# Two up projections of a decoder trunk, from plain 512-token products to 2x2 blocks with seven half-size products

## The chip, the cores and the metric

The kernel runs as one program on one core of a Trainium2 chip. The metric is the device time of that core in microseconds. TensorE (PE) multiplies, ScalarE (ACT) and VectorE (DVE) read PSUM and work elementwise, GpSimd (POOL) works elementwise on SBUF alone, SyncE (SP) issues nearly all transfers.

## The reference

A two-layer decoder trunk on 512 tokens with a model width of 1024, all in float32. Layer 0 mixes with block-sparse and dilated attention, layer 1 with stick-breaking attention; after each mixer comes a gated MLP, and after both x becomes LayerNorm(alpha * x + f(x)). What is changed is the first matrix product of the MLP in both layers (F = 2816):

```
def conv_ffn(h, w_up, conv_w, conv_b, w_down):
    u = h @ w_up                          # 512 x 1024 times 1024 x 5632
    up = pad(u, two rows of zeros in front)
    c = conv_b + sum over j of conv_w[j] * up[:, j:j + S]      # causal, width 3, per column
    g, val = c[..., :F], c[..., F:]
    return (silu(g) * val) @ w_down
```

## The kernel before

Every float32 product is three fp32r matmuls: each operand is split into a head (`w_hi`, `xt_hi`: the value rounded to fp32r) and a rest (`w_lo`, `xt_lo`: what the rounding left), and a product is hi*hi + lo*hi + hi*lo. The weights come as one stream of 1024 KB steps (two units of 128x1024), each into one of two buffers `w_raw`. For each step SP issues the load once POOL has made the rests of the step two before (`load`, L197), ACT copies the whole step into `w_hi` (`heads`, L301, one instruction at L305), and POOL subtracts twice 128x1024 into `w_lo` (`rest`, L242, L248). PE waits for each unit's rest.

The up projection keeps the activations transposed: `xt_hi` and `xt_lo` hold 8 chunks of 128 input columns by 512 tokens. There are 22 pairs f of a gate tile and a value tile, each 128 output columns by 512 tokens, one weight step for each pair. `col_unit` (L885, matmuls at L897) makes one tile with 8 chunks x 3 matmuls of 512 tokens, 48 for a pair. The first two pairs are cut into token halves of 256 (`first_columns` at L903, `up_half` at L1159), woven into the transposes of the norm before; `up_body` (L1149) does the other 20. Gates go to PSUM banks 0 and 2, values to 1 and 3. For each tile ACT makes the last tap and the bias from PSUM (L499, L505), DVE adds two more taps from PSUM (L795, L799), ACT takes a sigmoid (L503), and DVE multiplies twice (L805, L809) into `h_all`. ACT has in its order also the heads of the pair two ahead. The down projection then reads `h_all` in 11 chunks of two tiles (heads L490, rests L817) with matmuls at L866 into all eight banks; `row_tiles` (L845) takes the four token tiles of a chunk one after the other, 12 matmuls each.

Ahead of the up projection stands `norm` (L623): per token tile a sum (L576), statistics (L604 to L610), the scaled result (L596, L619), then PE transposes it (`turn_x`, L841) into PSUM, ACT copies heads (`xt_heads`, L314) and DVE makes rests (`xt_rests`, L564). Each engine's order is written out by hand; all waits are semaphores. ACT's queue issues the gains and shifts of the norm (`load_gain`, L309). No transfer is issued by POOL.

Of the kernel before, what the change touches and what calls it, by code (L numbers as in the profile page):

```python
# [22 lines left out]
F32 = mybir.dt.float32  # L23
# [38 lines left out]

WARM = (20, 5)


def build(nc, x_in, w_stream, ident_in, rope_in, mask_in, tri_in, conv_in, ln_in, out):
    ctx = ExitStack()
    with ctx:
# [13 lines left out]
        xt_lo = sb("xt_lo", [P, KD, S], F32R)  # L82
        a_hi = sb("a_hi", [P, KD, S], F32R)
        a_lo = sb("a_lo", [P, KD, S], F32R)
        x = sb("x", [P, NT, D])
        gain = sb("gain", [P, D])
# [25 lines left out]
        with ExitStack() as st:  # L112
            h_all = sb("h_all", [P, KF, S], stack=st)
            cg, cv, sig = ([sb(f"{n}0", [P, S], stack=st)] for n in ("cg", "cv", "sig"))
            sb("below_second", [P, S], stack=st)
            for n, tiles in (("cg", cg), ("cv", cv), ("sig", sig)):
                tiles.append(sb(f"{n}1", [P, S], stack=st))
        with ExitStack() as st:
# [43 lines left out]

        V = [Phase(f"v{l}", "rows act dve") for l in range(DEPTH)]
# [3 lines left out]
        N = [Phase(f"n{i}", "rows sum mean sq lv y0 va nt mulg xn scaled shifted") for i in range(2 * DEPTH)]  # L167
        T = [Phase(f"t{i}", "mm hi lo") for i in range(2 * DEPTH)]
        U = [Phase(f"u{l}", "g_mm cg cv g1 gc sg m1 v1 vc h") for l in range(DEPTH)]
# [10 lines left out]
        def filled(c, it):  # L180
            return 16 * (c // 2 + it + 1)


        @block.sync
        def _(sp):
# [11 lines left out]
            def load(c, it=0):  # L197

                sp.wait_ge(lo_ready, 2 * (c + 2 * it) - 2)
                sp.dma_start(w_raw[c % 2][:, :], w_stream[c + 2 * it]).then_inc(raw_full[c % 2], 16)  # L200

# [22 lines left out]
            with sp.Fori(0, (STEPS - ahead - 7) // 2) as it:  # L224
                for j in range(2):
                    load(ahead + 7 + j, it)
            for t in range(NT - 1):
                if t < 2:
                    sp.wait_ge(N[-1]["shifted"], t + 1)
# [11 lines left out]
        def _(pool):  # L241
            def rest(c, it=0):  # L242
                s = c % 2
                for u in range(2):

                    pool.wait_ge(hi_ready, 2 * (c + 2 * it) + u + 1)
# [14 lines left out]
            for l in range(DEPTH):  # L261
# [27 lines left out]
                with pool.Fori(0, (PER_LAYER - AT_UP - 2) // 2) as it:  # L289
                    for j in range(2):  # L290
                        rest(b + AT_UP + 2 + j, it)
                if (PER_LAYER - AT_UP) % 2:
                    rest(b + PER_LAYER - 1)
            for t in range(2):
                pool.wait_ge(N[-1]["scaled"], t + 1)
                pool.tensor_tensor(x[:, t, :], x[:, t, :], shift[:, :], ALU.add).then_inc(N[-1]["shifted"], 1)


        @block.scalar
        def _(act):  # L300
# [147 lines left out]
            for l in range(DEPTH):  # L448
# [32 lines left out]
                heads(b + AT_UP, used=False)  # L481
                for i, after in ((2 * l, b + AT_O + 4), (2 * l + 1, b + PER_LAYER)):
                    if i % 2:

                        def chunk_heads(c, it=0, used=True):
                            j = c + 2 * it
                            act.wait_ge(U[l]["h"], 2 * j + 2)
# [5 lines left out]
                        def up_body(c, it, first):  # L493
                            f, u = c + 2 * it, U[l]
                            s = c % 2
                            act.wait_ge(u["g_mm"], f + 1)
                            if not first:
                                act.wait_ge(u["h"], f - 1)
                            act.activation(cg[s][:, :], bank[2 * s][:, :], ACT.Identity,  # L499
                                           bias=tap(l, f, 3),  # L500
                                           scale=tap(l, f, 2)).then_inc(u["cg"], 1)
                            act.wait_ge(u["gc"], f + 1)
                            act.activation(sig[s][:, :], cg[s][:, :], ACT.Sigmoid).then_inc(u["sg"], 1)  # L503
                            act.wait_ge(w_used, b + AT_UP + f + 1)
                            act.activation(cv[s][:, :], bank[2 * s + 1][:, :], ACT.Identity,  # L505
                                           bias=tap(l, f + KF, 3),
                                           scale=tap(l, f + KF, 2)).then_inc(u["cv"], 1)
                            heads(b + AT_UP + c + 2, it)

                        act.preload_act_table(ACT.Sigmoid)  # L510
                        act.wait_ge(conv_full, 16)
                        up_body(0, 0, True)
                        up_body(1, 0, True)
                        chunk_heads(0, used=False)
                        with act.Fori(1, KF // 2) as it:
                            up_body(0, it, False)
                            up_body(1, it, False)
# [3 lines left out]
                        chunk_heads(1)  # L521
# [8 lines left out]
                    if i == 2 * DEPTH - 1:  # L530
                        def scaled(t):
# [3 lines left out]
                                           scale=stat[:, t, 8:9]).then_inc(N[i]["scaled"], 1)  # L535
# [7 lines left out]
                    else:  # L543
# [10 lines left out]
                        act.wait_ge(N[i]["xn"], NT)  # L554
                        load_gain(i + 1)
# [3 lines left out]
        def _(dve):  # L559
# [26 lines left out]
            def norm_mul(i, t):  # L586
# [7 lines left out]
                elif t >= 2:  # L594
                    dve.wait_ge(n["scaled"], t - 1)
# [170 lines left out]
            for l in range(DEPTH):  # L766
# [23 lines left out]
                def up_body(c, it):  # L790
                    f, u, s = c + 2 * it, U[l], c % 2

                    def convolve(ps, acc, tile, start, mid, end):
                        dve.wait_ge(start, f + 1)
                        dve.scalar_tensor_tensor(out=acc[:, 1:S], in0=ps[:, 0:S - 1],  # L795
                                                 scalar=tap(l, tile, 1), in1=acc[:, 1:S],
                                                 op0=ALU.mult, op1=ALU.add).then_inc(mid, 1)
# [465 lines left out]
```

## Time and profile before

| what | us |
|---|---|
| median of 3 runs (lowest 1241.75, highest 2036.46) | 1243.0 |
| the profiled execution, its own time | 1241.35 |
| its span, first to last instruction | 1239.5 |
| PE busy / PE weight load busy | 1219.1 / 1005.7 |
| DVE / ACT / POOL busy | 622.2 / 510.0 / 557.9 |

PE runs through the whole span. The matmul records overlap, since a matmul begins before the one before it has drained: the mean duration of a matmul is not its price, the distance between starts is. The highest of the three runs stands far off the other two, which agree with the profiled execution.

### The profile page before, as it was taken

What the parts mean: (1) busy time and instruction counts of PE and PEld (TensorE: products, weight loads), DVE (VectorE), ACT (ScalarE), POOL (GpSimd) and SP (SyncE); (2) the same over time, 40 slices, a digit from 0 to 9 for tenths busy, and PEclk for the clock granted to TensorE, in tenths of its full rate; (3) what the DMA queues carried; (4) which work ended last, traced back from release to release, by engine and by line L of the source; (5) the groups of instructions that cost most, each with busy time, mean ns of one, the idle gap of its engine ahead of it and who ended that gap; (6) DMA issues with size and microseconds to landing.
All of it is one profiled execution on the core that took longest, in us unless ns stands there. A gap on an engine that the chain in (4) does not pass through costs nothing.

```text
span 1239.5 us, 17100 instructions
## 1 busy us (share of the span) xinstructions
PE 1219.1 (98%) x6274; PEld 1005.7 (81%) x6274; DVE 622.2 (50%) x992; ACT 510.0 (41%) x747; POOL 557.9 (45%) x242
## 2 busy tenths in 40 slices
PE   9999999999999999999999999999999999999997
PEld 8877776789888888888888788878988888888885
DVE  2045656366666565612280355654765566662226
ACT  3245555454333333322342476754433333342223
POOL 4534544353555444455534333324444455444553
PEclk9999999999999999999999999999999999999999
DMA  8221212023222322222232211112222222222211
GB/s 297 102 85 61 93 60 95 34 103 136 89 83 99 102 102 102 101 80 90 102 113 94 91 50 63 68 69 102 102 103 102 102 81 88 101 102 102 102 68 68
DMA packets 20022, 117.25 MB, mean 95 GB/s; under 512 B 2448, under 2 KB 2832, under 8 KB 7568
## 3 DMA queue, kind: packets, MB, share of 16 engines
q1 hardware_dynamic: 18400, 112.21, 25.0%
q10 hardware_dynamic: 1584, 4.51, 1.1%
q8 instruction: 28, 0.46, 0.2%
q14 instruction: 10, 0.08, 0.0%
HBM read 110.41 MB, written 2.10 MB: 91 GB/s over the span
## 4 chain that ended last, share of the span: by engine, by line
PE 90%; DVE 3%; POOL 2%; ACT 2%; issue 1%; DVEq 0%; ACTq 0%
PE bank L897 52%; PE bank L866 29%; POOL w_lo L248 2%; PE bank L949 2%; PE bank L976 1%; PE bank L1035 1%; PE bank L1014 1%; PE bank L963 1%; ACT w_hi L305 1%; PE bank L841 1%; PE bank L1024 1%; PE bank L1069 1%; DVE probs L737 0%; DVE ln_mul L596 0%; DVE x L619 0%
## 5 line engine op out<-in xcount | busy, mean ns | idle before, releaser
L248 POOL TENSOR_TENSOR w_lo<-w_raw,w_hi 128x1024 fp32r<-128x1024 f32 x196 | 506.7, 2607 | 629.0 <-ACT w_hi L305 619.3
L897 PE MATMUL bank<-xt_hi,w_hi 128*128 128x512 f32 (+1 forms) x1056 | 396.3, 375 | 2.4 <-ACT v_all L335 1.7
L897 PE MATMUL bank<-xt_lo,w_hi 128*128 128x512 f32 (+1 forms) x1056 | 396.8, 376 | 0.0
L897 PE MATMUL bank<-xt_hi,w_lo 128*128 128x512 f32 (+1 forms) x1056 | 392.8, 372 | 0.0
L305 ACT ACTIVATE w_hi<-w_raw 128x2048 fp32r<-128x2048 f32 x97 | 185.3, 1910 | 205.4 <-PE bank L866 197.0
L897 PEld LDWEIGHTS bank<-xt_hi,w_hi 128*128 128x128 f32 x1056 | 198.9, 188 | 39.4 <-ACT v_all L335 2.4
L897 PEld LDWEIGHTS bank<-xt_lo,w_hi 128*128 128x128 f32 x1056 | 198.8, 188 | 38.8 <-issue 4.8
L897 PEld LDWEIGHTS bank<-xt_hi,w_lo 128*128 128x128 f32 x1056 | 198.7, 188 | 34.2
L866 PE MATMUL bank<-w_hi,a_hi 128*128 128x512 f32 x480 | 153.2, 394 | 3.5 <-POOL w_lo L248 1.9
L866 PE MATMUL bank<-w_hi,a_lo 128*128 128x512 f32 x480 | 151.8, 391 | 0.0
L866 PE MATMUL bank<-w_lo,a_hi 128*128 128x512 f32 x480 | 151.7, 391 | 0.0
L817 DVE TENSOR_TENSOR a_lo<-h_all,a_hi 128x1024 fp32r<-128x1024 f32 x22 | 53.0, 2407 | 150.1 <-ACT a_hi L490 150.1
L809 DVE TENSOR_TENSOR h_all<-sig,cv 128x512 f32 (+1 forms) x44 | 118.9, 2703 | 6.1 <-DVE cv L799 0.3
L866 PEld LDWEIGHTS bank<-w_hi,a_hi 128*128 128x128 f32 x480 | 88.8, 188 | 25.7 <-POOL w_lo L248 3.1
L866 PEld LDWEIGHTS bank<-w_lo,a_hi 128*128 128x128 f32 x480 | 90.1, 188 | 19.2 <-issue 0.4
L866 PEld LDWEIGHTS bank<-w_hi,a_lo 128*128 128x128 f32 x480 | 90.0, 188 | 19.2 <-issue 0.4
L499 ACT ACTIVATE cg<-bank,conv 128x512 f32<-128x512 f32 x44 | 34.2, 778 | 116.4 <-PE bank L897 116.2
L795 DVE SCALAR_TENSOR_TENSOR cv<-bank,conv,cv 128x511 f32<-128x511 f32 x44 | 33.0, 749 | 91.2 <-ACT cv L505 91.2
L505 ACT ACTIVATE cv<-bank,conv 128x512 f32<-128x512 f32 x44 | 34.2, 777 | 82.3 <-PE bank L897 82.2
L503 ACT ACTIVATE sig<-cg 128x512 f32<-128x512 f32 x44 | 27.8, 632 | 82.6 <-DVE cg L799 82.6
L795 DVE SCALAR_TENSOR_TENSOR cg<-bank,conv,cg 128x511 f32<-128x511 f32 x44 | 33.0, 749 | 41.0 <-ACT cg L499 41.0
L360 ACT ACTIVATE probs<-probs,sm 128x128 f32<-128x128 f32 (+3 forms) x64 | 35.4, 555 | 43.0 <-DVE sm L693 43.0
(90 smaller groups left out, 1147.4 us busy)
## 6 DMA issues: line engine op xcount, KB each, us to landing
w_raw<-w_stream SPq DMA_DIRECT2D x97, 1024.0 KB, 4.8
x<-x_in SPq DMA_DIRECT2D x4, 512.0 KB, 7.2
gain<-ln_in ACTq DMA_DIRECT2D x4, 512.0 KB, 4.0
shift<-ln_in ACTq DMA_DIRECT2D x4, 512.0 KB, 5.4
qs<-qc SPq DMA_DIRECT2D x16, 128.0 KB, 2.1
ks<-kc SPq DMA_DIRECT2D x16, 128.0 KB, 2.0
out<-x SPq DMA_DIRECT2D x3, 512.0 KB, 2.6
w_raw<-w_stream SPq DMA_DIRECT2D x2, 512.0 KB, 5.9
```

The costliest lines, as they stand in the source:

```text
L248: pool.tensor_tensor(w_lo[slot(c)][:, part], w_raw[s][:, part], w_hi[slot(c)][:, part].bitcast(F32), ALU.subtract).then_inc(lo_ready, 1)
L305: act.activation(w_hi[slot(c)][:, :], w_raw[c % 2][:, :], ACT.Copy).then_inc(hi_ready, 2)
L360: act.activation(e, e, ACT.Exp, bias=m[:, 0:1], scale=-1.0, accum_out=m[:, 1:2]).then_inc(a["ex"], 1)
L499: act.activation(cg[s][:, :], bank[2 * s][:, :], ACT.Identity, bias=tap(l, f, 3), scale=tap(l, f, 2)).then_inc(u["cg"], 1)
L503: act.activation(sig[s][:, :], cg[s][:, :], ACT.Sigmoid).then_inc(u["sg"], 1)
L505: act.activation(cv[s][:, :], bank[2 * s + 1][:, :], ACT.Identity, bias=tap(l, f + KF, 3), scale=tap(l, f + KF, 2)).then_inc(u["cv"], 1)
L795: dve.scalar_tensor_tensor(out=acc[:, 1:S], in0=ps[:, 0:S - 1], scalar=tap(l, tile, 1), in1=acc[:, 1:S], op0=ALU.mult, op1=ALU.add).then_i ...
L809: dve.tensor_tensor(h_all[:, bass.ds(f, 1), :], sig[s][:, :].rearrange("p (a q) -> p a q", a=1), cv[s][:, :].rearrange("p (a q) -> p a q", ...
L817: dve.tensor_tensor(a_lo[:, k:k + 2, :], h_all[:, bass.ds(2 * j, 2), :], a_hi[:, k:k + 2, :].bitcast(F32), ALU.subtract).then_inc(DN[l]["a ...
L866: mm = pe.matmul(bank[2 * t + g][:, :], lhs, w[s][:, u * UNIT + g * HALF:u * UNIT + (g + 1) * HALF], start=first and n == 0, stop=end and ...
L897: mm = pe.matmul(out_bank[:, tok], w, m, start=n == 0, stop=n == len(todo) - 1)
L949: mm = pe.matmul(bank[2 + h][:, k * P:(k + 1) * P], qa[par][part, qi * P:(qi + 1) * P], ka[par][part, k * P:(k + 1) * P], start=True, stop ...
```

## The change

For 20 of the 22 pairs of each layer (`FIRST` = 2 pairs stay as they are), gate tile and value tile are taken together as a 2x2 block product: the weight pair is split into low and high input half (4 chunks each) and into gate and value, the activations into low and high input half and left and right 256 tokens. Seven products of half size replace eight: 4 chunks x 3 matmuls of 256 tokens each, 84 for a pair. The operands of the seven are:

- weights: three as loaded (W11, W22, W12) and four sums. SUM_Q and SUM_1 are made by transfer: SP loads the fourth quarter of the step twice into `qs_raw`, and one transfer issued by POOL adds the first and the third quarter of the step to the copies while it writes (`accum_op=ALU.add`). SUM_2 and SUM_4 are made in PSUM banks 6 and 7: ACT copies W11 into bank 6, DVE adds SUM_1 in place, and then W12 into bank 7.
- tokens: two as they are, four mixed (`t_raw`, `t_hi`, `t_lo`) once per layer.
- results: ACT copies the first product out of bank 4 (`keep_first`), and DVE combines the seven into the gate and value banks with five instructions.

Weights' heads are now made in quarters of 128x512 by ACT, seven per pair; rests five per pair by POOL and two by DVE. The seven operands lie in the two `w_hi` and `w_lo` buffers, one place for each, so a head waits for the same product of the pair before (`freed`). The last multiplication of a pair moves from DVE to POOL (`gate`), sigmoid and its product become one Silu on ACT. A step of the stream is loaded as 768 KB and twice 256 KB, when POOL has made the last rest of the pair two before. In the first down chunk the token tiles are taken in the order 0, 2, 3, 1.

```diff
+            def load_after(c):
+                l, m = (c - 2) // PER_LAYER, (c - 2) % PER_LAYER - AT_UP - FIRST
+                if 0 <= m < NW:
+                    sp.wait_ge(*W[l].at("lo_p", 5 * m + 5))
...
+                l, m = c // PER_LAYER, c % PER_LAYER - AT_UP - FIRST
+                if 0 <= m < NW:
+                    sp.dma_start(w_raw[c % 2][:, 0:3 * Q], w_stream[c, :, 0:3 * Q]).then_inc(raw_full[c % 2], 16)
+                    if m == 0:
+                        sp.wait_ge(N[2 * l]["xn"], NT)
+                    for n in range(2):
+                        sp.dma_start(qs_raw[m % 2][:, n, :], w_stream[c, :, 3 * Q:4 * Q]).then_inc(qs_full[m % 2], 16)
...
+                def token_sum(j):                                  # POOL
+                    pool.wait_ge(T[2 * l + 1]["lo"], 2 * j + 2)
+                    pool.tensor_tensor(x_raw[:, j, :, :], xt_hi[:, :, j * P:(j + 1) * P].bitcast(F32),
+                                       xt_lo[:, :, j * P:(j + 1) * P].bitcast(F32), ALU.add).then_inc(w["x"], 1)
...
+                def add_weights(m):
+                    s = m % 2
+                    pool.wait_ge(qs_full[s], 2 * summed(l, m))
+                    pool.dma_start(qs_raw[s][:, :, :],
+                                   w_stream[b + AT_UP + FIRST + m, :, 0:4 * Q]
+                                   .rearrange("p (a b q) -> p a b q", a=2, b=2)[:, :, 0, :],
+                                   accum_op=ALU.add).then_inc(qs_sum[s], 16)
...
+                for m in range(NW):                                # POOL, for each pair
+                    raw = w_raw[(b + AT_UP + FIRST + m) % 2]
+                    w_rest(m, W11, raw[:, 0:Q])
+                    w_rest(m, SUM_Q, qs_raw[m % 2][:, 0, :])
+                    gate(m)
+                    if m + 1 < NW:
+                        add_weights(m + 1)
+                    w_rest(m, W22, raw[:, 2 * Q:3 * Q])
+                    w_rest(m, SUM_1, qs_raw[m % 2][:, 1, :])
+                    w_rest(m, W12, raw[:, Q:2 * Q])
+                gate(KF - 2)
+                rest(b + AT_DN)
...
+                        def up_body(c, it, first=False, again=True):        # ACT
+                            m, par = c + 2 * it, c % 2
+                            raw, q_s = w_raw[(b + AT_UP + FIRST + c) % 2], qs_raw[par]
+                            if not first:
+                                keep_first(m - 1, again)
+                                freed(m, W11)
+                            act.wait_ge(raw_full[(b + AT_UP + FIRST + c) % 2], filled(b + AT_UP + FIRST + c, it))
+                            w_head(W11, raw[:, 0:Q])
...
+                            act.activation(bank[6][:, :], raw[:, 0:Q], ACT.Copy).then_inc(w["a6"], 1)
+                            act.wait_ge(qs_sum[par], summed(l, c, it))
...
+                            w_head(SUM_Q, q_s[:, 0, :])
+                            silu(m, par)
...
+                            w_head(W22, raw[:, 2 * Q:3 * Q])
+                            act.wait_ge(*w.at("s", 2 * m + 2))
+                            w_head(SUM_2, bank[6][:, :])
...
+                            w_head(SUM_1, q_s[:, 1, :])
...
+                                value_combined(m - 1, 1 - par)
...
+                            w_head(W12, raw[:, Q:2 * Q])
...
+                            w_head(SUM_4, bank[7][:, :])
+                            if not first:
+                                gate_combined(m - 1, 1 - par)
...
+                def up_body(c, it, level=2):                       # DVE
+                    m, par = c + 2 * it, c % 2
+                    n, other = m - 1, 1 - par
+                    if level > 1:
+                        gates_combined(m - 2, par)
+                    if level > 0:
+                        value_taps(m, par)
+                        gate_taps(m, par)
+                        w_rest(n, SUM_4, bank[7])
+                    dve.wait_ge(qs_sum[par], summed(l, c, it))
+                    second_sum(m, c)
+                    if level > 0:
+                        early_products(n)
+                    dve.wait_ge(raw_full[(b + AT_UP + FIRST + c) % 2], filled(b + AT_UP + FIRST + c, it))
+                    fourth_sum(m, c)
+                    if level > 0:
+                        values_combined(n, other)
+                    w_rest(m, SUM_2, bank[6])
...
+                tokens_mixed(0)                                    # DVE, once per layer
+                tokens_mixed(1)
+                for j in range(2):
+                    t_rest(T2, j, bank[5 + 2 * j][:, :].rearrange("p (k q) -> p k q", k=4), 4 * j + 2)
+                    t_rest(T1, j, t_raw[:, T1, :, j * P:(j + 1) * P], 4 * j + 3)
+                gate_taps(0, 0)
+                value_taps(0, 0)
...
+                def product(e, tokens, out):                       # PE
+                    s, part = operand(l, e)
+                    for k in range(4):
+                        at = slice(part.start + k * P, part.start + (k + 1) * P)
+                        for v, (lhs, rhs) in enumerate(((w_hi, tokens[0]), (w_hi, tokens[1]), (w_lo, tokens[0]))):
+                            mm = pe.matmul(out, lhs[s][:, at], rhs[:, k, :], start=(k, v) == (0, 0),
+                                           stop=(k, v) == (3, 2))
```

On PE the seven products of a pair stand in the order W11, SUM_Q, SUM_2, W22, SUM_1, W12, SUM_4; W22 waits for POOL's third rest of the pair, SUM_1 for the fourth, W12 for the fifth.

## Rows read from the trace of the kernel before

**Rows 1.** The page: the engines' busy time, and the granted clock in 40 slices.
```profile
PE 1219.1 (98%) x6274; PEld 1005.7 (81%) x6274; DVE 622.2 (50%) x992; ACT 510.0 (41%) x747; POOL 557.9 (45%) x242
PEclk9999999999999999999999999999999999999999
```
**Rows 2.** The chain that ended last, in order of time: start us, us, what.
```profile
271.69 2.83 PE bank L897 x24
275.39 5.71 PE bank L897 x48
...
282.21 232.08 PE bank L897 x1080
```
**Rows 3.** Busy time by stretches: stretch, length, then PE, PEld, DVE, ACT, POOL, clock, DMA.
```profile
296.38:514.30 217.92, 217.92 (x963) 180.47 (x962) 134.21 (x122) 81.03 (x82) 106.38 (x41) 1.00 0.28 98
514.30:612.00 97.70, 97.52 (x430) 80.41 (x430) 26.09 (x12) 27.83 (x20) 50.08 (x18) 1.00 0.27 95
```
**Rows 4.** POOL by line: min/median/max ns, first and last start.
```profile
L248 POOL TENSOR_TENSOR w_lo<-w_raw,w_hi x196: 2368/2402/3427, 6.6 to 1212.5; 128x1024 fp32r<-128x1024 f32 x196
L258 POOL TENSOR_TENSOR qa<-qc,qs x8: 1272/1274/1618, 28.6 to 210.3; 128x512 f32<-128x512 f32 x8
```
**Rows 5.** SP's loads of weights, 300 to 500 us: the issue, and issue to landing.
```profile
L200 SPq DMA_DIRECT2D w_raw<-w_stream x18: 332/333/333, 304.6 to 489.9; - x18
DMA to landing us min/median/max: 4.7/4.8/4.9
```
**Rows 6.** POOL in order of time, from 262 us: start, us, what, idle before.
```profile
273.65 5.88 POOL L248 TENSOR_TENSOR w_lo<-w_raw,w_hi 128x1024 fp32r<-128x1024 f32 x2 [12.20 <-ACT w_hi L305]
...
299.22 5.21 POOL L248 TENSOR_TENSOR w_lo<-w_raw,w_hi 128x1024 fp32r<-128x1024 f32 x2 [0.52 <-ACT w_hi L305]
```
**Rows 7.** SP in order of time: the first load issued in the loop.
```profile
304.60 33.33 SPq L200 DMA_DIRECT2D w_raw<-w_stream  x4
```
**Rows 8.** ACT's queue issuing the gains and shifts: min/median/max ns.
```profile
L309 ACTq DMA_DIRECT2D gain<-ln_in x4: 339/343/1391, 16.5 to 877.6; - x4
L309 ACTq DMA_DIRECT2D shift<-ln_in x4: 450/616/869, 18.0 to 878.0; - x4
```
**Rows 9.** The page's transfers: KB each, median us to landing.
```profile
masks<-mask_in SPq DMA_DIRECT2D x1, 512.0 KB, 12.7
out<-x SPq DMA_DIRECT2D x3, 512.0 KB, 2.6
```
**Rows 10.** ACT by line: a copy from PSUM, and a copy of twice the size.
```profile
L314 ACT ACTIVATE xt_hi<-bank x32: 579/594/617, 8.5 to 878.1; 128x512 fp32r<-128x512 f32 x32
L490 ACT ACTIVATE a_hi<-h_all x22: 1039/1039/1066, 302.2 to 1209.9; 128x1024 fp32r x16, 128x1024 fp32r<-128x1024 f32 x6
L499 ACT ACTIVATE cg<-bank,conv x44: 759/778/782, 288.0 to 1104.4; 128x512 f32<-128x512 f32 x44
L503 ACT ACTIVATE sig<-cg x44: 631/632/633, 290.5 to 1107.0; 128x512 f32<-128x512 f32 x44
```
**Rows 11.** DVE by line: with an operand in PSUM, and with both in SBUF (L809).
```profile
L564 DVE TENSOR_TENSOR xt_lo<-bank,xt_hi x32: 678/681/693, 9.2 to 878.8; 128x512 fp32r<-128x512 f32 x32
L795 DVE SCALAR_TENSOR_TENSOR cv<-bank,conv,cv x44: 735/750/752, 291.8 to 1110.8; 128x511 f32<-128x511 f32 x44
L809 DVE TENSOR_TENSOR h_all<-sig,cv x44: 692/2866/2881, 293.4 to 1112.6; 128x512 f32 x40, 128x512 f32<-128x512 f32 x4
```
**Rows 12.** DVE groups by shape: count, busy us, mean ns, idle before.
```profile
L740 DVE TENSOR_TENSOR probs<-bank,probs 128x256 f32<-128x256 f32 x8 | 3.4, 424 | 0.3
```
**Rows 13.** DVE in order of time, in the last tile of the norm.
```profile
277.37 2.18 DVE L607 SCALAR_TENSOR_TENSOR stat<-stat 128x1 f32<-128x1 f32 x1
...
279.78 1.28 DVE L619 SCALAR_TENSOR_TENSOR x<-ln_mul,stat,shift 128x1024 f32<-128x1024 f32 x1
...
282.88 1.29 DVE L564 TENSOR_TENSOR xt_lo<-bank,xt_hi 128x512 fp32r<-128x512 f32 x2 [0.62 <-ACT xt_hi L314]
```
**Rows 14.** ACT in order of time, after the last transposed tile.
```profile
283.54 1.28 ACT L510 ACT_TABLE_LOAD   x1 [0.20 <-issue]
```

More of the change, by code:

```diff
@@ L61, with whole @@
 EARLY = (24, 12)
+FIRST = 2
+NW = KF - FIRST
+Q = 4 * P
+TOK = S // 2
+W11, SUM_Q, SUM_2, W22, SUM_1, W12, SUM_4 = range(7)
+HEADS = (W11, SUM_Q, W22, SUM_2, SUM_1, W12, SUM_4)
+T3, T2, T4, T1 = range(4)
+def whole(c):
+    return c - NW * ((c >= AT_DN) + (c >= PER_LAYER + AT_DN))
 WARM = (20, 5)
@@ L85, in build @@
         x = sb("x", [P, NT, D])
+        with ExitStack() as st:
+            qs_raw = [sb(f"qs_raw{s}", [P, 2, Q], stack=st) for s in range(2)]
         gain = sb("gain", [P, D])
@@ L223, in _ @@
             swaps(7)
-            with sp.Fori(0, (STEPS - ahead - 7) // 2) as it:
-                for j in range(2):
-                    load(ahead + 7 + j, it)
+            for c in range(ahead + 7, STEPS):
+                load_after(c)
             for t in range(NT - 1):
                 if t < 2:
-                    sp.wait_ge(N[-1]["shifted"], t + 1)
+                    sp.wait_ge(N_LAST["shifted"], t + 1)
                 else:
@@ new lines, in _ @@
+                        silu(KF - 2, 0)
+                        down_first = b + AT_DN
+                        act.wait_ge(raw_full[down_first % 2], filled(down_first, 0))
+                        for g in range(2):
+                            act.wait_ge(*w.at("p", 6 * last + 2 * g + 2))
+                            part = slice(g * UNIT, (g + 1) * UNIT)
+                            act.activation(w_hi[slot(down_first)][:, part], w_raw[down_first % 2][:, part],
+                                           ACT.Copy).then_inc(hi_ready, 1)
@@ new lines, in t_rest, with w_rest @@
+                def t_rest(row, j, src, seen):
+                    part = slice(j * P, (j + 1) * P)
+                    dve.wait_ge(*w.at("th", seen))
+                    dve.tensor_tensor(t_lo[:, row, :, part], src[:, :, :], t_hi[:, row, :, part].bitcast(F32), ALU.subtract).then_inc(w["tl_v"], 1)
+                def w_rest(m, e, src):
+                    s, part = operand(l, e)
+                    dve.wait_ge(*w.at("hi", 7 * m + HEADS.index(e) + 1))
+                    dve.tensor_tensor(w_lo[s][:, part], src[:, :], w_hi[s][:, part].bitcast(F32),
+                                      ALU.subtract).then_inc(w["lo_v"], 1)
@@ L1147, in _ @@
                           turning(2 * l + 1))
[L1149 to L1157 removed]
+                w, u = W[l], U[l]
```

343 lines of the change are left out of this document (268 added, 75 removed).

## The prediction

> **What bounds the kernel now.** I read the page first: PE is busy 98% of the span at a granted clock of nine tenths or more throughout, the level of 2.4 GHz, every other engine at most half of it [rows 1]. Then the chain of waits in order of time: in the up projection it is PE without a break, 232.08 us for 1080 matmuls [rows 2]. 120 of these are half-size (256 tokens), 960 full. Two pieces ahead price the half-size ones by themselves: 24 in 2.83 us and 48 in 5.71 us, so 0.118 to 0.119 us each; then the full ones take (232.08 - 14.2) / 960 = 0.227 us. The busy times by stretch say the same: 217.92 us for the 20 pairs that change, 10.9 us a pair, and PE is busy in all of it, and the down projection begins at once behind them [rows 3]. So only work taken from PE there, or waits given to it, moves the time. POOL is busy 106 us of those 218, DVE 134, ACT 81 [rows 3].
>
> **PE's work.** A pair goes from 48 x 0.227 = 10.9 us to 84 x 0.1185 = 9.95 us: 0.94 us less, 37.7 us for 40 pairs, 3.0% at best. The half-size price is measured on matmuls with the same three operand forms, across changes of bank. The Trainium skill (TensorE: Matmul & The Clock Gate, Back-to-back issue gap) gives about 81 ns for a sustained matmul of 128 columns and 131 ns for one of 512. My estimate from it is about 98 ns for 256, so 84 of them would cost 8.2 us against 6.3 us for 48 large ones, and the change would lose. By that rule the trace does not agree: 118 against 227 ns, almost in proportion to the columns, and the trace decides.
>
> **The other engines, a pair.** DVE: six instructions on 512 columns with one operand in PSUM at 0.68 [rows 11], four taps at 0.75 [rows 11], three on 256 at 0.42 [rows 12]: 8.4 us, and some 0.6 us of waits on itself. ACT: nine copies, eight at 0.60 and one on half the columns at about 0.4, one Silu at 0.63, two taps at 0.78 [rows 10]: 7.4 us. POOL: six subtractions or products on 512 columns at 1.27 [rows 4] are 7.6 us, and the issue of one transfer. All fit below 9.95, DVE narrowly. Two SBUF operands on DVE collide with POOL (0.69 became 2.87 [rows 11]), but in the loop DVE now always has one in PSUM.
>
> What doesn't fit is a **ring through POOL and the transfers**. POOL finishes W12's rest of pair m, the last; that lets SP load pair m+2. POOL goes on with W11, SUM_Q and gate of pair m+1 (3.8 us) and then must wait in add_weights(m+2) until these loads have landed. Only behind it come the rests W22, SUM_1 and W12 of pair m+1, and the last of them lets the next load go. So one pair can't take less than:
> - POOL's end to SP's issue, 0.17: POOL ends 299.22 + 5.21 = 304.43, SP issues at 304.60 [rows 6, 7];
> - issue to landing of 1024 KB, 4.8 [rows 5], and 256 KB more. Over the stretch the transfers moved 98 GB/s at a share of 0.28 [rows 3], so 350 GB/s at full share: 0.75;
> - the issue on POOL's queue, s. No transfer is issued by POOL in this trace. Below, SP's issue of 0.33 [rows 5]; above, a POOL instruction on as many elements as it adds, 2.4 [rows 4]. ACT's queue issued up to 0.87 and 1.39 [rows 8]; I take 1.0, between these, since they are the nearest: an issue on the queue of a computing engine;
> - three rests, 3.82 [rows 4], and about 0.1 between them.
>
> That is 9.64 + s = **10.64 us** a pair, PE's 9.95 being smaller. The Trainium skill (DMA: Bandwidth & Descriptors, Latency and other measured facts) puts a first byte of about 1 us on this path, the emission by the Q7 cores; with it the ring would be the same.
>
> A second ring: the accumulating transfer (a, from issue to landing), ACT's SUM_Q head 0.60, POOL's SUM_Q rest and gate 2.55, waits 0.15, the next issue: a + 3.3 + s. It decides only from a = 6.35. For a, below stands 512 KB in 2.6, above the 12.7 of a transfer in a full queue [rows 9]; I take 4.8, as for 1024 KB [rows 5], since the sum must also read what it adds to.
>
> **Start of each layer.** POOL ends its rests at 273.65 + 5.88 = 279.53 [rows 6], and now takes token_sum(0), 128x1024 from SBUF, 2.4 us. DVE's L619 starts at 279.78 [rows 13] with two SBUF operands; it must wait as L607 did in that place (2.18 for 0.2 [rows 13]). The last x row, its transposes and rests come 2.1 us late: the last rests end at 286.3 instead of 284.2 [rows 13]. PE, which had nothing between, reaches the changed pairs at 298.5, not 296.38 [rows 3]. Meanwhile ACT has its last heads (two at 0.6) and the table load of 1.28 [rows 14], and copies at 287.5. DVE mixes tokens (eight at 0.68 plus waits, 6.0), makes four rests (2.8 to 3.5), taps (3.0), two sums (1.4), ACT makes SUM_2's head (0.6), DVE its rest (0.7): PE's third product can't start before 302.4, though PE could at 301.3. On POOL gate(0) waits for the taps (299.7), then come the gate 1.3, the issue 1.0 and three rests of 1.27 (ACT's heads for them, up to 304.5 for the last, are just in time), and some 0.5 of waits between engines: POOL's last rest of pair 0 ends at about **306.5**. From there 19 rings, and behind the last two products of 1.42: the up projection ends at 306.5 + 19 x 10.64 + 2.8 = 511.5, where it ended at 514.3 [rows 3].
>
> **End of each layer.** The weights of the first down chunk share the operands' places and stand on POOL behind gate(KF-2). POOL's last rest ends 2.8 before PE is through; a gate of 1.3 and two rests of 2.4 [rows 4] are done 0.9 and 3.3 after it, the second wanted at 2.3. DVE's a_lo(0), with both operands in SBUF beside POOL, is late by as much. I count **2.5 us** (1 to 4), where before there was no idle time. The order 0, 2, 3, 1 covers the last taps, and the later chunks (10.9 us of PE each) cover theirs. The issue of the gains at another place, the longer code and SP's wait for the norm cost nothing: the queues have nothing due then; without that cover each would be below 1 us.
>
> **Sum.** Per layer 511.5 + 2.5 - 514.3 = -0.3; for two -0.6. Against the profiled execution's 1241.35 that is **1241 us**; its span of 1239.5 and the 1.85 around it stay together, and the median of the runs shown is 1243.0, 1.65 above it. Nearly all of the 37.7 us goes back: 2 x 19 x 0.69 = 26 to the ring, 2 x (306.5 + 2.8 - 296.4 - 9.95) = 6 to the start, 5 to the end. In general the difference is 2 x (19 T - 202.5) for a period T.
>
> **Rivals.**
> 1. *PE stays the bound.* Issue at SP's price, s = 0.33, gives a ring of 9.97: 2 x (189.4 - 202.5) = -26, 1215 us; with PE's own start some 1217. For it: the issues on SP and ACT are mostly short [rows 5, 8]. Against: they are issued by other queues. 16%.
> 2. *The accumulating transfer lands late*, slower. Place: ACT's wait for qs_sum ahead of SUM_Q, behind which POOL's SUM_Q, gate and next issue stand. At the middle of the bounds, a = 7.65, T = 11.95 and the time is 1241 + 49 = 1290. It decides from 6.35 and costs over 2% from a = 7.1. For it: it reads HBM and SBUF and writes, beside 1280 KB of loads in each pair; the load must restart for each. Against: 1024 KB needs 4.8. The Trainium skill (Collectives: The Full Stack, The bandwidth ceiling) says that the adding transfers run at half the rate, since they read two sources; no row here shows it. 20%.
> 3. *A dear issue.* s = 2.4: T = 12.04, 1294 us; over 2% from s = 1.75. POOL would be at 7.6 + 2.4 = 10 us of work, all in line with the load. 12%.
> 4. *DVE or the waits of PE.* DVE has 9.0 of 9.95; in rings of 10.64 it has room, but 0.15 more on each of its thirteen instructions makes 11.0, and so 1254. Fifteen waits a pair on PE in place of four may open gaps; at the changes of tile now none is seen. 7%.
>
> The forecast, a POOL ring of 10.2 to 11.2, has 45%: 1224 to 1262 by itself.
>
> **Range and chances.** About 2% is what a measurement of this kernel can tell from no change, so 1218 and 1268 are the borders. Faster: rival 1 with a good start and end, and a little of the forecast's edge, 17%. Slower: most of rivals 2 and 3 and a part of 4, 31%. Within: 52%. The range takes in rival 1 and the lower half of 2 and 3: 1216 to 1286.
>
> **What would show it.** In the trace after: half-size matmuls 0.118 apart; periods of about 10.6 us; PE idle 0.7 us a pair ahead of W22, put down to POOL's w_lo; POOL idle about 2 us ahead of its transfer, released by the loads; L619 in the norm's last tile 2 us longer; the down projection 2 to 3 us after the up. It is wrong if POOL is never idle (rival 3), if ACT's SUM_Q head waits long for a transfer and POOL for ACT (rival 2), or if PE has no idle time (rival 1).

## The result, and the profile after

The changed kernel takes **1259.8 us** (median of four runs, 1258.5 to 1260.0), against 1242.4 for the kernel before, run beside it: a ratio of 1.014, interval 1.012 to 1.016. It is slower by 17 us where 1241 us, no change, was forecast; the range of 1216 to 1286 held it. The profiled execution has 1260.03 us and a span of 1258.2, 18.7 more than before.

The page after, to be held beside [rows 1] and [rows 9]:

```profile
PE 1202.1 (96%) x7714; PEld 1055.4 (84%) x7714; DVE 681.9 (54%) x1288; ACT 620.2 (49%) x1089; POOL 723.7 (58%) x458
...
PEclk9999999998999999999999999999999999999999
...
qs_raw<-w_stream SPq DMA_DIRECT2D x80, 256.0 KB, 4.8
qs_raw<-w_stream POOLq DMA_DIRECT2D x40, 512.0 KB, 5.6
```

PE is busy 17 us less, in 19 us more span: it is no longer what the time goes by. No other engine is near its limit either; POOL has 58%. A kernel in which no engine is full is held by waits, and the up projection of layer 0 shows which (stretch, length, then busy time of PE, PEld, DVE, ACT, POOL, clock, DMA), to be held beside the first row of [rows 3]:

```profile
303.70:523.25 219.55, 206.19 (x1683) 202.58 (x1681) 154.41 (x261) 130.87 (x240) 175.03 (x140) 1.00 0.62 163
250.00:300.00 50.00, 45.69 (x284) 41.42 (x283) 38.76 (x60) 23.86 (x41) 27.53 (x13) 0.93 0.33 104
```

The second row is the stretch ahead of it; before, PE was busy 49.86 of these 50 us at a clock of 1.00. The waits between 300 and 525 us say who holds whom (engine and line, what it waited for: us in all, times, longest):

```profile
ACT w_hi L637 <- DMA qs_raw<-w_stream: 75.7, 19, 5.4
DVE bank L1097 <- DMA qs_raw<-w_stream: 58.9, 18, 4.5
POOL qs_raw L374 <- DMA qs_raw<-w_stream: 41.4, 18, 3.5
PEld bank L1494 <- issue: 15.4, 17, 2.1
PE bank L1494 <- POOL w_lo L383: 13.4, 18, 1.9
...
POOL w_lo L383 <- ACT w_hi L637: 1.7, 8, 0.3
```

PE waits for POOL's rests once a pair, POOL for SP's transfers once a pair. ACT too waits long for a transfer, the adding one (75.7 us), but POOL hardly waits for ACT (1.7 us), so this wait is not what holds POOL. One turn in order of time, first SP, then POOL (start, us, what, idle before):

```profile
400.01 0.33 SPq L262 DMA_DIRECT2D w_raw<-w_stream  x1
400.38 0.91 SPq L266 DMA_DIRECT2D qs_raw<-w_stream  x2
411.07 0.33 SPq L262 DMA_DIRECT2D w_raw<-w_stream  x1
```
```profile
406.17 1.09 POOL L374 DMA_DIRECT2D qs_raw<-w_stream  x1 [2.32 <-DMA qs_raw<-w_stream]
406.95 1.63 POOL L383 TENSOR_TENSOR w_lo<-w_raw,w_hi 128x512 fp32r<-128x512 f32 x1
408.20 1.61 POOL L383 TENSOR_TENSOR w_lo<-qs_raw,w_hi 128x512 fp32r<-128x512 f32 x1
409.43 2.87 POOL L383 TENSOR_TENSOR w_lo<-w_raw,w_hi 128x512 fp32r<-128x512 f32 x2
```

SP issues at 400.01. POOL stands idle 2.32 us and may issue at 406.17, when the copies are there: 6.16. Then come its issue and three rests, W12 being the first of the two at 409.43, and SP issues again 4.90 after POOL did. That is the ring of the prediction, its terms in the order in which it named them. (POOL's records overlap: starts, or ends, of its rests are 1.23 to 1.26 apart where one record is 1.6 long, so the distance is the price of a rest, not the record.)

### The profile page after: what moved, and what is told of

It reads as the page before. It is cut to its first block, busy times and chain, and to the rows that moved or that the text cites. A ratio compares the mean times of both kernels' runs of the same rounds, so it can differ in the third digit from the quotient of the medians.

```text
span 1258.2 us, 20328 instructions
## 1 busy us (share of the span) xinstructions
PE 1202.1 (96%) x7714; PEld 1055.4 (84%) x7714; DVE 681.9 (54%) x1288; ACT 620.2 (49%) x1089; POOL 723.7 (58%) x458
## 4 chain that ended last, share of the span: by engine, by line
PE 51%; POOL 17%; DMA 14%; DVE 9%; ACT 3%; issue 3%; SPq 2%; DVEq 0%; ACTq 0%; POOLq 0%
PE bank L1195 27%; DMA qs_raw<-w_stream 14%; PE bank L1226 13%; POOL w_lo L383 11%; POOL qs_raw L374 3%; POOL w_lo L315 2%; PE bank L1494 2%; PE bank L1278 2%; PE bank L1305 1%; PE bank L1364 1%; PE bank L1343 1%; PE bank L1292 1%; ACT w_hi L425 1%; SPq L266 1%; DVE x L849 1%
## 5 line engine op out<-in xcount | busy, mean ns | idle before, releaser
L315 POOL TENSOR_TENSOR w_lo<-w_raw,w_hi 128x1024 fp32r<-128x1024 f32 x116 | 299.0, 2599 | 370.5 <-ACT w_hi L425 360.9
L1494 PE MATMUL bank<-t_hi,w_hi 128*128 128x256 f32 x640 | 184.6, 288 | 25.3 <-POOL w_lo L383 25.3
L1494 PE MATMUL bank<-t_lo,w_hi 128*128 128x256 f32 x640 | 181.0, 283 | 0.0
L1494 PE MATMUL bank<-t_hi,w_lo 128*128 128x256 f32 x640 | 180.9, 283 | 0.0
L383 POOL TENSOR_TENSOR w_lo<-w_raw,w_hi 128x512 fp32r<-128x512 f32 x120 | 179.2, 1610 | 0.5 <-ACT w_hi L637 0.5
L1226 PE MATMUL bank<-xt_hi,w_hi 128*128 128x512 f32 (+1 forms) x416 | 148.6, 357 | 2.4 <-ACT v_all L455 1.7
L1226 PE MATMUL bank<-xt_lo,w_hi 128*128 128x512 f32 (+1 forms) x416 | 149.0, 358 | 0.0
L1226 PE MATMUL bank<-xt_hi,w_lo 128*128 128x512 f32 (+1 forms) x416 | 145.0, 349 | 0.0
L1494 PE MATMUL bank<-xt_hi,w_hi 128*128 128x256 f32 x480 | 135.8, 283 | 0.0
L1494 PE MATMUL bank<-xt_lo,w_hi 128*128 128x256 f32 x480 | 135.8, 283 | 0.0
```

Of the source, the lines that this page charges most:

```text
L315: pool.tensor_tensor(w_lo[slot(c)][:, part], w_raw[s][:, part], w_hi[slot(c)][:, part].bitcast(F32), ALU.subtract).then_inc(lo_ready, 1)
L383: pool.tensor_tensor(w_lo[s][:, part], src, w_hi[s][:, part].bitcast(F32), ALU.subtract).then_inc(w["lo_p"], 1)
L1226: mm = pe.matmul(out_bank[:, tok], w, m, start=n == 0, stop=n == len(todo) - 1)
L1494: mm = pe.matmul(out, lhs[s][:, at], rhs[:, k, :], start=(k, v) == (0, 0), stop=(k, v) == (3, 2))
```

## The experiments

All run beside the kernel before; "after" is the changed kernel's 1259.8 us. The medians of the ring are taken over the 18 turns of each layer, from SP's first issue for a pair to POOL's issue, and from there to SP's next: after 6.07 and 6.02 in the two layers, 6.03 together, and 4.91; a whole turn is 10.95. (There are 18 turns and not 20: the first transfer in the loop finds its copies landed, and behind the last pair but one POOL issues none.)

**1. More bytes in the same load (e1_load_full).** If the ring holds the time, what is added to the transfers must come out in every pair.

```diff
-sp.dma_start(w_raw[c % 2][:, 0:3 * Q], w_stream[c, :, 0:3 * Q])
+sp.dma_start(w_raw[c % 2][:, 0:4 * Q], w_stream[c, :, 0:4 * Q])
```

> SP's first load of each changed pair is made 1024 KB in place of 768 KB (the fourth quarter isn't read by anyone); it stands ahead of the two 256 KB loads that POOL waits for. Ring theory (the period is POOL's last rest, the loads of the pair two ahead, POOL's issue and three rests: 11.05 us in the changed kernel): 256 KB more pass ahead of the landing, 0.6 to 0.75 us a pair, so 18 rings in each of two layers add 22 to 27 us: 1282 to 1287 us. Rival (the accumulating transfer's landing or an engine sets the period): under 0.2 us a pair, 1260 to 1267 us.

Measured 1273.3 us, 1.0252 (1.0235 to 1.0269), 13.5 more than after. The turn in POOL's records:

```profile
397.90 1.09 POOL L374 DMA_DIRECT2D qs_raw<-w_stream  x1 [2.54 <-DMA qs_raw<-w_stream]
409.24 1.09 POOL L374 DMA_DIRECT2D qs_raw<-w_stream  x1 [2.50 <-DMA qs_raw<-w_stream]
```

The ring's medians are 6.37 + 4.90 = 11.3: all of the 0.34 more is in the wait for the loads, and 0.34 in each of 36 turns is 12 us of the 13.5. So the ring is confirmed. Its slope isn't: 256 KB more in long rows cost a third of a microsecond, less than half of the 0.75 that I had taken for 256 KB, and the time stayed below the 1282 expected.

**2. The two copies ahead of the 768 KB (e2_copies_first).** POOL's issue needs only the copies; the large load has time until then. This leaves every byte in place and changes only what the ring waits for.

```diff
+                    def main():
+                        sp.dma_start(w_raw[...][:, 0:3 * Q], w_stream[c, :, 0:3 * Q])...
                     if m == 0:
+                        main()
                         sp.wait_ge(N[2 * l]["xn"], NT)
                     for n in range(2):
                         sp.dma_start(qs_raw[m % 2][:, n, :], ...)
+                    if m > 0:
+                        main()
```

> Same wait and same bytes, but SP issues the two 256 KB loads ahead of the 768 KB one (but for the first pair of a layer). Ring theory: the copies land some 2 us earlier, POOL's idle time of 2.3 us before its issue goes, the ring falls to about 9.3 us, below PE's 9.95; 18 x 1.1 x 2 = 40 us less: 1219 to 1226 us, and W11's head may now come nearer to its load. Rival (the accumulating transfer's landing sets it, or DVE or the half-size matmuls do): the period stays at 10.8 to 11.1 and the time at 1252 to 1262 us.

Measured **1230.3 us**, 0.9904 (0.9888 to 0.9921): 29.5 below after, and 1% faster than before. SP, then POOL:

```profile
400.97 0.80 SPq L268 DMA_DIRECT2D qs_raw<-w_stream  x2
401.82 0.43 SPq L263 DMA_DIRECT2D w_raw<-w_stream  x1
```
```profile
396.02 1.09 POOL L378 DMA_DIRECT2D qs_raw<-w_stream  x1 [0.85 <-DMA qs_raw<-w_stream]
406.06 1.09 POOL L378 DMA_DIRECT2D qs_raw<-w_stream  x1 [1.27 <-DMA qs_raw<-w_stream]
```

From SP's issue to POOL's it is now 5.09 (medians 5.02 and 4.95 in the two layers), the ring 9.9 to 10.0, POOL idle half as long. The change's whole loss hangs on the order of three lines. 1.0 us for each of 36 turns would be 36, and 34 to 41 were expected; 30 came. PE is nearly full now (149.4 of the 150 us between 330 and 480) and needs 10.08 a pair (e5 below), which leaves 0.87 in 36 turns, 31 us. Against that the start of the down projection has become dearer: PE waits there for DVE's rests, 3.2 us in each layer where it was 0.8 and 1.1 in after.

```profile
PE bank L1199 <- DVE a_lo L1133: 3.2, 2, 1.6
```

**3. The transfer without its addition (e3_no_adding).** Rival 2: does the accumulating transfer delay anybody? The kernel leaves the two sums out, so it no longer computes the product and is of use for the time alone.

```diff
-                                   .rearrange(...)[:, :, 0, :],
-                                   accum_op=ALU.add).then_inc(qs_sum[s], 16)
+                                   .rearrange(...)[:, :, 0, :]).then_inc(qs_sum[s], 16)
```

> POOL's transfer copies the same bytes and doesn't add: the sums SUM_Q and SUM_1 are left out. Ring theory: POOL's issue and the loads are as before, the landing of this transfer has 2.3 us of slack: period 10.8 to 11.1, 1252 to 1262 us; a part of the 0.4 us that the landing of the copies has too much may go if the adding transfer was in the way of the loads. Rival (adding transfers land late and hold the period): the landing falls from 5.5 to about 3.5 us and the period by 1 us, 1220 to 1230 us.

Measured 1250.2 us, 1.0065 (1.0048 to 1.0082), 9.6 below after.

```profile
402.20 0.74 POOL L374 DMA_DIRECT2D qs_raw<-w_stream  x1 [2.39 <-DMA qs_raw<-w_stream]
...
412.78 0.75 POOL L374 DMA_DIRECT2D qs_raw<-w_stream  x1 [2.27 <-DMA qs_raw<-w_stream]
```

The page has its landing at 3.7 us instead of 5.6:

```profile
qs_raw<-w_stream POOLq DMA_DIRECT2D x40, 512.0 KB, 3.7
```

That much earlier, and POOL still idles 2.3 us: the landing that it waits for is SP's, not its own. The loads take the same 6.02 (6.03 after). What got shorter is POOL's part, 4.57 for 4.91, and the issue alone does it: 0.745 us for 1.089. 0.35 in 36 turns would be 13, and from the first turn of a layer to its last the rests do gain 6.1 and 6.8 us; 9.6 were measured, because the start of the down projection gives 3.6 back (PE's idle time there goes from 1.3 and 1.5 to 3.2 a layer, as in e2). So rival 2 is refuted, and the adding costs through its issue.

**4. The token sums out of the norm's way (e4_token_sums_late).** POOL's two sums of 128x1024 begin only when the norm is done.

```diff
+                    if j == 0:
+                        pool.wait_ge(N[2 * l]["xn"], NT)
```

> POOL starts its two token sums only when DVE has made the last row tile of x. Collision theory (DVE's two instructions with SBUF operands waited 2.2 and 2.1 us for POOL's token sums in each layer): the last x tile comes 4.2 us earlier, the granted clock stays at its upper level; the token sums end near 287 and DVE's mixing waits for them up to 1 us: each layer starts 3 to 4 us earlier, 1251 to 1254 us. Rival (the start is set by the tail of mixing, rests and taps, which then waits for the sums): under 1 us a layer, 1258 to 1260 us.

Measured 1249.7 us, 1.0058 (1.0042 to 1.0075), 10.2 below after, a little more than expected. In DVE's order of time, after:

```profile
278.35 2.18 DVE L837 SCALAR_TENSOR_TENSOR stat<-stat 128x1 f32<-128x1 f32 x1
280.56 2.30 DVE L840 SCALAR_TENSOR_TENSOR stat<-stat 128x1 f32<-128x1 f32 x1
282.90 3.33 DVE L849 SCALAR_TENSOR_TENSOR x<-ln_mul,stat,shift 128x1024 f32<-128x1024 f32 x1
```

and with the edit (the same two instructions, two lines further down):

```profile
280.65 0.16 DVE L842 SCALAR_TENSOR_TENSOR stat<-stat 128x1 f32<-128x1 f32 x1
280.85 1.28 DVE L851 SCALAR_TENSOR_TENSOR x<-ln_mul,stat,shift 128x1024 f32<-128x1024 f32 x1
```

I had counted one collision there; there were two. POOL's records and PE's in the kernel after show both ends:

```profile
280.47 4.67 POOL L361 TENSOR_TENSOR x_raw<-xt_hi,xt_lo 128x1024 f32<-128x1024 f32 x2
```
```profile
286.28 1.97 PE L1170 MATMUL bank<-ident,x 128*128 128x128 f32 x8 [4.19 <-DVE x L849]
```

L840 works on one column and yet waits out the first token sum, L849 the second: 4.2 us instead of my 2.1. PE then stood idle for 4.19, and the granted clock of the stretch was 0.93, so for a part of it at the level of 1.2 GHz, and the eight transposes behind the idle time took 1.97 us where eight took 1.03 before it; with the edit PE is busy 49.76 of the same 50 us at 1.00:

```profile
250.00:300.00 50.00, 49.76 (x337) 45.50 (x336) 39.63 (x66) 26.55 (x45) 31.79 (x17) 1.00 0.33 105
```

The Trainium skill (SBUF — State Buffer, Who interferes with whom) says that a DVE instruction with two SBUF inputs contends with a GpSimd instruction that reads SBUF, and that the order of issue, not the form of the instruction, decides who is blocked. The trace agrees, down to an instruction of one column: 2.30 us beside POOL, 0.16 without.

**5. Copies first, and early (e5_copies_first_and_early).** The copies' place is free one rest sooner (SUM_1's) than the large load's (W12's). SP waits for the fourth rest to issue the copies, for the fifth to issue the rest.

```diff
+                if 0 <= m < NW - 2:
+                    sp.wait_ge(*W[l].at("lo_p", 5 * m + 4))      # then the two copies
...
+                        sp.wait_ge(*W[l].at("lo_p", 5 * before + 5))   # then main()
```

> As the kernel with the copies first (1230.3 us, POOL still idle about 1.1 us before its issue, period 10.03), and SP waits for POOL's fourth rest of the pair two before (SUM_1, the last reader of the copies), not the fifth; the 768 KB load still waits for the fifth. Ring theory: the ring loses another 1.27 us and is below PE's 9.95 us; 18 x 0.08 x 2 = 3 us less: 1226 to 1229 us, POOL idle under 0.3 us before its issue, PE without idle time inside a layer's 20 pairs. Rival (what is left is not this ring: the landing of the adding transfer, DVE): 1230 to 1232 us.

Measured 1228.9 us, 0.9897 (0.988 to 0.9913), 31.0 below after. The stretch of 150 us inside layer 0's up projection:

```profile
330.00:480.00 150.00, 150.00 (x1252) 150.00 (x1252) 116.15 (x195) 104.28 (x179) 130.22 (x106) 1.00 0.73 187
```
```profile
399.81 1.06 POOL L383 DMA_DIRECT2D qs_raw<-w_stream  x1
409.87 1.07 POOL L383 DMA_DIRECT2D qs_raw<-w_stream  x1
```

PE has no idle time and POOL waits for nothing ahead of its issue. The ring is gone as the bound; a pair takes 10.08, which is 84 matmuls at 0.120. POOL works 8.7 us of it, DVE 7.8, ACT 7.0 (their busy times over 150 us, times 10.08), where 8.6, 8.4 and 7.4 were predicted: the engines' terms hold, DVE's and ACT's a little high. It is 1.5 us better than e2, and the intervals overlap: PE was the bound there already, nearly.

**6. One issue for both copies (e6_one_issue).** Is it the row of three issues on SP that makes the landing late?

```diff
-                    for n in range(2):
-                        sp.dma_start(qs_raw[m % 2][:, n, :], w_stream[c, :, 3 * Q:4 * Q])...
+                    sp.dma_start(qs_raw[m % 2][:, :, :], w_stream[c, :, None, 3 * Q:4 * Q]
+                                 .broadcast_to([P, 2, Q])).then_inc(qs_full[m % 2], 16)
...
-                    pool.wait_ge(qs_full[s], 2 * summed(l, m))
+                    pool.wait_ge(qs_full[s], summed(l, m))
```

> The changed kernel, but SP makes both copies by one transfer of 512 KB whose source is read twice (a broadcast axis). Same bytes, one issue of 0.43 us less. If the 0.4 us by which the landing was under-priced is the serial issue of three transfers, the period falls by 0.4 us to 10.65 and the time by 15 us to 1245 us (1242 to 1248). Rival (it is the bytes in rows of 2 KB, or the queue): under 0.1 us a pair, 1256 to 1262 us.

Measured 1258.6 us, 1.0133 (1.0116 to 1.015), 1.2 below after, which is no difference to speak of.

```profile
398.03 0.33 SPq L262 DMA_DIRECT2D w_raw<-w_stream  x1
398.40 0.43 SPq L265 DMA_DIRECT2D qs_raw<-w_stream  x1
```
```profile
404.06 1.09 POOL L374 DMA_DIRECT2D qs_raw<-w_stream  x1 [1.98 <-DMA qs_raw<-w_stream]
```

SP is done issuing half a microsecond sooner, and the copies are there after 6.03 as before (medians 6.03 and 6.00). The issues are not the cause.

**7. POOL's issue behind W22's rest (e7_issue_after_w22).** The same ring broken at another link: no load is touched, POOL only does one rest while it would have waited.

```diff
                     gate(m)
+                    w_rest(m, W22, raw[:, 2 * Q:3 * Q])
                     if m + 1 < NW:
                         add_weights(m + 1)
-                    w_rest(m, W22, raw[:, 2 * Q:3 * Q])
```

> The changed kernel with POOL's W22 rest ahead of its issue, nothing else. Ring theory: only two rests stand behind the issue in the ring, so the first ring falls by 1.25 us to 9.8; the second ring (adding transfer 5.5 from issue, ACT's head 0.65, SUM_Q, gate and W22 3.8) comes to 10.0 and takes over: period 9.95 to 10.2, 18 x 0.95 x 2 = 34 us less: 1222 to 1230 us. Rival (POOL's order doesn't matter because bytes or another engine bound it): 1252 to 1262 us.

Measured 1228.6 us, 0.9898 (0.9882 to 0.9915), 31.2 below after. The stretch of 150 us, and two of its waits:

```profile
330.00:480.00 150.00, 150.00 (x1250) 149.79 (x1250) 114.28 (x194) 97.01 (x180) 128.93 (x106) 1.00 0.69 183
```
```profile
ACT w_hi L637 <- DMA qs_raw<-w_stream: 47.1, 15, 3.8
...
POOL w_lo L383 <- ACT w_hi L637: 20.4, 15, 1.6
```

The second copy lands as late as in after (5.76 from SP's first issue, 5.74 after), but POOL has work until then, and nobody on the path cares. POOL waits for ACT now, by the second ring; what that costs stays below PE's 10.08 a pair. This is the clearest test of the theory: bytes, transfers, issues and instructions are all the same, one line stands one place lower, and the whole loss of the change is gone.

**8. Both repairs (e8_early_and_late_sums)**: the edits of e5 and e4 together.

> Copies first and early, and the token sums only behind the last x tile. The ring's gain (29.5 us measured for the copies first, 3 more expected) and the start's (10.2 us measured) are at different places and add up: 1216 to 1219 us, faster than both kernels. Rival (the start's gain was taken from time in which the first ring would have waited anyway): 1222 to 1228 us.

Measured 1218.4 us, 0.9812 (0.9796 to 0.9829): 10.4 below e5, where e4 alone gave 10.2. The two costs add up. A wait that is left stands where the down projection begins, in PE's order of time:

```profile
501.66 0.70 PE L1206 MATMUL bank<-w_hi,a_hi 128*128 128x512 f32 x2 [1.63 <-DVE a_lo L1140]
...
514.38 0.72 PE L1206 MATMUL bank<-w_hi,a_hi 128*128 128x512 f32 x2 [1.57 <-DVE a_lo L1140]
```

**9. And the start of the down projection (e9_and_down_start).** In e8's kernel ACT makes the first chunk's heads between the two halves of the first down weights, and the heads of the second weights and of the next chunk ahead of the last pair's gate; POOL makes the rest of the second weights ahead of the last gate, DVE the first chunk's rests ahead of the last values.

```diff
+                            if g == 0:
+                                chunk_heads(0, used=False)          # ACT
...
+                        heads(down_first + 1, used=False)
+                        chunk_heads(1, used=False)
                         gate_combined(last, 1)
                         silu(KF - 1, 1)
...
+                rest(b + AT_DN + 1)                                 # POOL
                 gate(KF - 1)
...
+                chunk_rests(0)                                      # DVE
                 values_combined(last, 1)
```

> The last kernel (copies first and early, late token sums, 1218.4 us), and the start of the down projection reordered: ACT makes the heads of the first tiles between the two halves of the first weights, the second weights' heads and the second tiles' heads ahead of the last gate tap; POOL makes the second weights' rests ahead of the last gate; DVE makes the first tiles' rests ahead of the last value combination. In the kernel before it PE stood 1.6 us for the first tiles' rests and 1.5 us for the second ones in each layer. If these waits are what they seem, both shrink to under 0.5 us: 2 x 2 to 2.6 us less, 1213 to 1215 us. Rival (the wait goes over to the first weights' rests on POOL or to the last taps, which now come later): 1216 to 1219 us.

Measured **1211.8 us**, 0.9756 (0.9742 to 0.9769), 6.7 below e8, more than expected, and the best of all: faster than both kernels. PE is busy 98% again, with fewer matmul microseconds than before:

```profile
PE 1187.5 (98%) x7714; PEld 1048.7 (87%) x7714; DVE 676.8 (56%) x1288; ACT 638.5 (53%) x1089; POOL 723.3 (60%) x458
```

The wait of PE's matmuls for DVE's rests of the down chunks, over the whole kernel (us, times, longest), first in e8, then here; the one for POOL's weight rests stays at 2.3 us in both:

```profile
PE bank L1206 <- DVE a_lo L1140: 6.8, 6, 1.6
```
```profile
PE bank L1208 <- POOL w_lo L324: 2.3, 4, 0.7
...
PE bank L1208 <- DVE a_lo L1142: 0.4, 2, 0.2
```

## Why the prediction was wrong

**The mechanism was right**, and the time was missed all the same. Each predicted sign is there: half-size matmuls 0.12 apart, POOL idle 2.3 us ahead of its transfer and released by SP's loads (predicted: about 2), PE idle 13.4 us in 18 pairs for POOL's `w_lo` (0.74 a pair, predicted 0.7), L849 late, the down projection late. ACT's SUM_Q head did wait long for the adding transfer, but POOL did not wait for ACT, and it takes both for rival 2; POOL was never full. What failed is the size of one term in the ring, and one count at the start.

- *PE's price* (0.1185): 0.120 where PE has no gaps, so 10.08 a pair for 9.95. Right to 1.3%; it doesn't count in after, where PE waits, and is 5 us in e9.
- *Issue to landing of the loads*, 4.8 + 0.75 = 5.55, with POOL's issue at once behind it: **6.03** from issue to issue. This is the step that failed, and it failed in two parts. The smaller is the landing itself: 5.74 us from SP's first issue to the landing of the second copy. I took the 1024 KB row [rows 5] and added the bytes at the rate of full traffic [rows 3]. Three transfers, two of them in rows of 2 KB, don't add up so. By e1, 256 KB more in long rows cost 0.34, so the bytes alone would make the landing 5.1, not 5.74; and the copies land only after 4.7 even when they go first (e2). Of the excess, e6 rules out the number of issues, e3 rules out the addition and its slower landing. Whether it is the short rows or the number of transfers in flight stays open: no run changed the row length at equal bytes. The larger part is a term that the sum put at nothing: POOL doesn't issue when the copies land but 0.29 us later, in the median of the turns of after, e1, e2 and e6 alike. In the turn shown, SP issues the second copy at 400.86; it lands 5.0 us later, at 405.88, and POOL's issue starts at 406.17. The four copies issued from 400 to 412 us:

```profile
DMA to landing us min/median/max: 4.7/4.9/5.0
```
- *POOL's part*, s = 1.0 with the three rests 3.82, 0.1 between and 0.17 to SP: 5.09 predicted, 4.91 measured. The issue alone is 1.09, so the choice among 0.33, 1.0 and 2.4 was good; SP follows POOL's end in 0.04, not 0.17.
- The *median ring* is thus 10.95 for 10.64, and 0.31 us count 18 times a layer: 5.6 us. (I had counted 19 rings; the last pair has no transfer to wait for and takes what PE needs. From POOL's last rest of the pair before it, the up projection ends 13.7 us later in both layers, where a ring and two products made 13.4, so the wrong count cost only 0.6 us in all, by luck.) In layer 0 two turns took 12.2, the first and the fourth, 2.5 more together. With the smaller excess of layer 1 (two turns of 11.8 and 11.4) the rings are worth 15 us: (509.7 - 309.9) / 18 is 11.10 in layer 0, 11.01 in layer 1.
- *Start of a layer*: POOL's last rest of pair 0 ends at 309.9, that is 308.9 on the clock of before, since the norm already came 1.0 later; predicted 306.5. The miss is 2.4, and 1.8 in layer 1. A count failed here: two instructions of DVE waited where I let one wait, and PE, idle for 4.2 us, had 0.93 of its clock around it. I had read [rows 13] for L619 only; L610 ahead of it stands in the same place and has two SBUF operands too. e4 gives back 5.1 a layer, more than the miss, since my 2.1 was in the sum.
- *End of a layer*, 2.5 each: 1.65 and 2.0, within the 1 to 4 that I gave.
- *The norm* already comes 1.0 us later in layer 0 of this execution, ahead of everything that was changed, which no step of mine has. It was lost in the attention, where the granted clock was lower for a while; the same stretch before, then after:

```profile
207.00:220.00 13.00, 10.14 (x92) 7.18 (x89) 8.87 (x32) 7.77 (x19) 5.16 (x5) 1.00 0.29 103
```
```profile
207.00:220.00 13.00, 11.13 (x90) 8.28 (x86) 8.00 (x27) 6.82 (x19) 5.18 (x5) 0.87 0.28 103
```

  PE idles 1.67 us up to 212.6 in both. In e5 and e9, which have the change too, this stretch has a clock of 1.00 and the norm comes 0.1 later, so the microsecond doesn't belong to the change. Why the clock fell in some of these kernels and not in others is open.

Together, against a span that I had 0.6 below that of before: rings 15.0, starts 4.2, last pairs 0.6, ends -1.35, norm 1.0; that is 19.4 for a miss of 18.7 + 0.6 = 19.3.

**The rivals.** Rival 1 (PE stays the bound, 1215 to 1217) rested on the smaller issue price, which is refuted; PE did become the bound once the ring was broken, in e5 and e7 (1229), and with start and end mended the time was 1212. Rival 2 is refuted by e3: a = 5.5 stands below its point of 6.35. The Trainium skill (Collectives: The Full Stack, The bandwidth ceiling) explains the half rate of a ReduceScatter by the second source that its add has to read. Here an adding transfer lands in 5.6 us where a plain one takes 3.7, half as long again and not twice as long, and with time to spare. Rival 3 needed an issue from 1.75. Rival 4 is refuted by e5: with DVE at 7.8 of 10.08, PE has no idle time.

The formula that I gave, 2 x (19 T - 202.5), turns 0.3 us of T into 11 us. The forecast's own range for T, 10.2 to 11.2, did hold 10.95; the single value was set at its lower half by adding bytes to a measured row.

## What to carry to other kernels

When no engine is full after a change, write the ring down: who waits for what, in which order of one queue, until it comes back to itself. Every term of it counts once a turn, so its least certain term, here a transfer's landing that was composed from another's, with nothing for the way from the landing to the waiting engine's next instruction, deserves a range of its own multiplied by the number of turns. And a ring is broken by order before it is broken by speed: what the blocked queue waits for goes first among its transfers, or independent work goes ahead of the blocking instruction.

## What was not expected of the hardware

- **A transfer's issue holds a computing engine's queue, by its kind.** On POOL the adding transfer took 1.089 us, the same without addition 0.745; on SP, issues of the same tile 0.43. In 36 turns the difference was worth up to 12 us.
- **Between the landing of a transfer and the issue that waits for it on POOL stand 0.29 us**, in the median of the turns of after, e1, e2 and e6. It counts in every turn of a ring.
- **A DVE instruction of one column waits as long as a large one** if both its inputs are in SBUF and POOL is reading there: 2.30 us for 0.16.
- **An idle PE of 4.2 us ahead of a stage goes with more than 4.2 us**: the granted clock of the 50 us was 0.93, a part of them at the level of 1.2 GHz, and the first changed product started at 303.78, with e4 at 297.41, 6.4 us earlier. POOL's last rest of that pair, from which the ring counts, gained 5.0.
- **Two turns of a layer are longer than the rest**: the first and the fourth in layer 0, 12.21 and 12.20 after, where the others lie at 10.8 to 11.1; 12.7 and 12.4 in e1, 10.6 and 10.7 in e7. In layer 1 after, the second and the tenth take 11.8 and 11.4. The fourth of layer 0 has SP's issue of the copies at 2.93 us in place of 0.91:

```profile
344.33 2.93 SPq L266 DMA_DIRECT2D qs_raw<-w_stream  x2
```

  The first has no such issue, so that isn't the whole cause; it stays open.
